# The gate product and the rotary rotation of a recurrent/attention layer given from GpSimd to VectorE

## The reference

```python
# recurrent branch, for each of two directions
r = sigmoid(einsum(xc, w_r) + b_r)            # xc: 4-tap convolution of x_rnn
i = sigmoid(einsum(xc, w_i) + b_i)
log_a = -8 * r * softplus(-lam);  a = exp(log_a)
u = sqrt(-expm1(2 * log_a)) * (i * xc)        # "gate times input" is i * xc
h = linear_scan(a, u)                         # h[t] = a[t] * h[t-1] + u[t]
# attention branch: 12 heads of 64; the first 16 columns of each head of q and k are rotated
rotated = concat([t1 * c - t2 * s, t2 * c + t1 * s])      # t1, t2: 8 columns each
```

## Time and profile before

| | us |
|---|---|
| median of 3 runs | 1599.41 |
| profiled execution, its own time | 1598.67 |
| its span, first to last instruction | 1596.9 |
| TensorE matmuls busy | 1550.0 (97%) |
| VectorE busy | 848.5 (53%) |
| ScalarE busy | 476.2 (30%) |
| GpSimd busy | 58.3 (4%) |
| mean granted clock of TensorE | 0.993 |

### The profile page before, as it was taken

One profiled execution on the slowest core, in us unless ns is written; L12 is line 12 of the kernel. 1 busy time (PEld: TensorE's weight loads), 2 busy tenths in 40 slices (PEclk: granted clock), 3 DMA queues, 4 the chain that ended last, 5 costly groups with the idle time before them and its releaser, 6 DMA issues.

```text
span 1596.9 us, 29275 instructions
## 1 busy us (share of the span) xinstructions
PE 1550.0 (97%) x12168; PEld 848.9 (53%) x12168; DVE 848.5 (53%) x1762; ACT 476.2 (30%) x699; POOL 58.3 (4%) x43
## 2 busy tenths in 40 slices
PE   6999999999999989999999999999999999999997
PEld 5877788888887877853433333333333333333332
DVE  5877676556687766744534345246245344443352
ACT  5577665444456966420000000000000000000001
POOL 0130000000003200010000000000000000000000
PEclk9999999999999999999999999999999999999998
DMA  9434365544443333559999999999999999999994
GB/s 385 152 145 149 115 226 189 205 184 184 185 172 132 136 155 108 199 197 416 399 384 425 408 386 410 404 386 420 395 402 416 371 423 415 382 414 412 384 409 188
DMA packets 66960, 473.78 MB, mean 297 GB/s; under 512 B 7408, under 2 KB 7664, under 8 KB 10768
## 3 DMA queue, kind: packets, MB, share of 16 engines
q1 hardware_dynamic: 64480, 460.88, 72.8%
q0 software_dynamic: 1920, 10.09, 1.8%
q10 hardware_dynamic: 432, 0.96, 0.2%
HBM read 469.80 MB, written 2.10 MB: 296 GB/s over the span
## 4 chain that ended last, share of the span: by engine, by line
PE 80%; DVE 9%; ACT 7%; issue 3%; DMA 1%; SPq 0%; DVEq 0%; ACTq 0%
PE bank L1298 26%; PE turn L1310 12%; PE mid L1298 10%; PE turn L1316 6%; PE bank L512 5%; PE bank L514 5%; PE bank L513 5%; DVE w_lo L507 2%; PE mid L512 2%; PE mid L514 2%; PE mid L513 2%; ACT w_hi L500 2%; DVE xT L1558 1%; DMA raw<-in_stream 1%; PE mid L1138 1%
## 5 line engine op out<-in xcount | busy, mean ns | idle before, releaser
L1298 PE MATMUL bank<-raw,gT 128*32 128x512 f32 (+1 forms) x4096 | 439.0, 566 | 0.7 <-ACT gT L957 0.7
L507 DVE TENSOR_TENSOR w_lo<-raw,w_hi 128x1024 fp32r<-128x1024 f32 x202 | 254.0, 1268 | 153.6 <-ACT w_hi L500 151.8
L1298 PEld LDWEIGHTS bank<-raw,gT 128*32 128x32 f32 x4096 | 135.4, 110 | 275.6 <-issue 266.4
L512 PE MATMUL bank<-w_hi,a_hi 128*128 128x512 f32 (+1 forms) x608 | 242.4, 399 | 15.2 <-DVE w_lo L507 12.0
L500 ACT ACTIVATE w_hi<-raw 128x1024 fp32r<-128x1024 f32 x202 | 211.2, 1056 | 127.3 <-PE bank L514 81.1
L514 PE MATMUL bank<-w_hi,a_lo 128*128 128x512 f32 (+1 forms) x608 | 234.9, 386 | 0.0
L513 PE MATMUL bank<-w_lo,a_hi 128*128 128x512 f32 (+1 forms) x608 | 234.6, 386 | 0.0
L1774 DVE STREAM_TRANSPOSE hT<-eh 32x128 f32<-32x128 f32 (+1 forms) x768 | 219.8, 286 | 24.2
L1310 PE MATMUL turn<-raw,hT 128*32 128x512 f32 x1792 | 213.1, 592 | 0.0
L1298 PE MATMUL mid<-raw,gT 128*32 128x256 f32 (+1 forms) x2048 | 189.0, 486 | 0.0
L983 ACT ACTIVATE eh<-bank 128x512 f32<-128x512 f32 (+1 forms) x32 | 17.4, 544 | 546.9 <-PE bank L1298 318.6
(11 more groups left out here) (240 smaller groups left out, 1323.7 us busy)
## 6 DMA issues: line engine op xcount, KB each, us to landing
raw<-in_stream SPq DMA_DIRECT2D x436, 1024.0 KB, 7.2
wg<-in_gates POOLq DMA_DIRECT2D x2, 2048.0 KB, 10.5
gain<-in_norms POOLq DMA_DIRECT2D x4, 512.0 KB, 4.1
x<-in_x SPq DMA_DIRECT2D x2, 512.0 KB, 6.5
raw<-in_stream SPq DMA_DIRECT2D x2, 512.0 KB, 6.5
tokens<-xs POOLq DMA_DIRECT2D x1, 1024.0 KB, 4.3
out_x<-xn SPq DMA_DIRECT2D x4, 256.0 KB, 2.2
const<-in_consts ACTq DMA_DIRECT2D x1, 752.0 KB, 11.6
```

The source lines that it names most:

```text
L507: nc.vector.tensor_tensor(w_lo[:, h % H, :], raw[:, part % R, lo:lo + HALF], w_hi[:, h % H, :].bitcast(F32), ALU.subtract).then_inc(lo_rea ...
L512: nc.tensor.matmul(out_, s_hi, wh, start=start, stop=False)
L1298: ins = nc.tensor.matmul(bank_[strip(s_), 0:w], gT[:, kt, strip(t_)], w_c, start=kt == 0, stop=kt == KT - 1)
```

## The change

The product `ig * xc` leaves GpSimd and becomes a step `lx` of VectorE. It stands at gaps 8.5, 11, 14.5 and 17 (with `le`, and half a gap later in the third block). The rotation becomes three steps of VectorE: two products at gap 11, two at 11.5, the subtraction and the addition at 14. The semaphores that were waited for by GpSimd are waited for by VectorE. GpSimd keeps its loads. Each operation keeps its shape.

```diff
@@ schedule
-        at(10, ("evac", ("qkv", 2)), ("rope",))
+        at(10, ("evac", ("qkv", 2)))
+        for i, gap in enumerate((11, 11.5, 14)):
+            at(gap, ("rope", i))
...
             at(tanh, ("la", d, hf))
+            at(decay + (d == 1 and hf == 0) / 2, ("lx", d, hf))
             at(decay, ("le", d, hf))
@@ gpsimd block
-                elif s[0] == "la":
-                    _, L, d, hf = s
-                    n = slice(4 * hf, 4 * hf + 4)
-
-                    pool.wait_ge(mid_free, mid_before(L, d * 4 + 2 * hf + 1)[1] + 4)
-                    nc.gpsimd.tensor_tensor(ig[:, n, :], ig[:, n, :], xc[:, n, :],
-                                            ALU.mult).then_inc(ix_ready, 1)
-                elif s[0] == "rope":
...
-                    for o, (a, c) in zip(tmp, ((t1, cb), (t2, sb_), (t2, cb), (t1, sb_))):
-                        nc.gpsimd.tensor_tensor(o, a, c, ALU.mult).then_inc(rope_s, 1)
-                    pool.wait_ge(rope_s, 4 * (L + 1))
-                    nc.gpsimd.tensor_tensor(t1, tmp[0], tmp[1], ALU.subtract).then_inc(rope_done, 1)
-                    nc.gpsimd.tensor_tensor(t2, tmp[2], tmp[3], ALU.add).then_inc(rope_done, 1)
@@ vector block
+                elif kind == "lx":
+                    _, L, d, hf = s
+                    n = slice(4 * hf, 4 * hf + 4)
+                    dve.wait_ge(mid_free, mid_before(L, d * 4 + 2 * hf + 1)[1] + 4)
+                    nc.vector.tensor_tensor(ig[:, n, :], ig[:, n, :], xc[:, n, :], ALU.mult).then_inc(ix_ready, 1)
+                elif kind == "rope":
+                    _, L, i = s
+                    z = qk[:, :, :].rearrange("p b (h w) -> p b h w", w=DH)
+                    NH = QK // DH
+                    t1, t2 = z[:, :, :, 0:8], z[:, :, :, 8:16]
+                    cb = cos.rearrange("p b (o k) -> p b o k", o=1).to_broadcast([P, TB, NH, 8])
+                    sb_ = sin.rearrange("p b (o k) -> p b o k", o=1).to_broadcast([P, TB, NH, 8])
...
+                    if i == 0:
+                        for n in range(3):
+                            evacuated(dve, (L, ("qkv", n)))
+
+                        bank_read(dve, TURN[("tx", L, 1)] + 1)
+                        bank_read(dve, TURN[("tx", L, 1)])
+                    if i < 2:
+                        for o, (a, c) in list(zip(tmp, ((t1, cb), (t2, sb_), (t2, cb), (t1, sb_))))[2 * i:2 * i + 2]:
+                            nc.vector.tensor_tensor(o, a, c, ALU.mult).then_inc(rope_s, 1)
+                    else:
+                        dve.wait_ge(rope_s, 4 * (L + 1))
+                        nc.vector.tensor_tensor(t1, tmp[0], tmp[1], ALU.subtract).then_inc(rope_done, 1)
+                        nc.vector.tensor_tensor(t2, tmp[2], tmp[3], ALU.add).then_inc(rope_done, 1)
```

More of the change, by code:

```diff
@@ L1535, in _ @@
                                 dve.wait_ge(chain, links[0])
+                elif kind == "lx":
[10 more added lines that the diff above has]
+                    sb_ = sin.rearrange("p b (o k) -> p b o k", o=1).to_broadcast([P, TB, NH, 8])
+                    flat = xn[:, :, :].rearrange("p b w -> p (b w)")
+                    W = TB * NH * 8
+                    tmp = [flat[:, j * W:(j + 1) * W].rearrange("p (b h k) -> p b h k", b=TB, k=8)
+                           for j in range(4)]
+                    if i == 0:
[10 more added lines that the diff above has]
+                        nc.vector.tensor_tensor(t2, tmp[2], tmp[3], ALU.add).then_inc(rope_done, 1)
                 elif kind == "lb":
```

## The result

| | before | after |
|---|---|---|
| median, us | 1599.41 (6 runs) | 1588.97 (6 runs, 1587.20 to 1589.35) |
| ratio, 95% interval | | 0.9930 (0.9917 to 0.9943) |
| profiled execution, its own time | 1598.67 | 1588.84 |
| its span | 1596.9 | 1587.0 |
| VectorE busy | 848.5 | 841.9 |

The changed kernel is 10.4 us faster by the medians and 9.9 us by the two spans; 9.8 were forecast. Lines of VectorE's code have moved: the forward scans are line 1562 now, the backward ones 1566, `w_lo` is 510, `root` 1547.

A forecast was written before the change was run, and what follows sets the result against it. A chain of waits between engines was taken to bound each layer's recurrence, TensorE the stage after. Savings of 4.76 and 5.01 us, together 9.77, with additions covered, gave a median of 1589.6 us; range for 8 in 10: 1586.5 to 1593.5.

The forecast's parts named there:

- Who makes the scans long: Recurrence: GpSimd's SBUF reads and VectorE's two-input instructions exclude each other; four forward scans take 4.65 us, backward ones 2.43.
- Removed: VectorE's excess leaves the chain: first scans 2.28, ScalarE's wait 0.18 or 0.43, second scans 2.16, third block's `root` 0.14 us.
- Added: New VectorE work per layer: four gate products at 1.225 us and six rotation operations on 384 elements at 0.55 us.
- The scattered row: VectorE row with a scattered operand, 0.40 us above the plain one; its share would make a rotation operation 0.85 us.
- GpSimd's price: Rival, rotation dear on VectorE: at GpSimd's 1.30 us each 1592.0 us, at 1.87 each 1596.6 us; chance 0.07.
- Where it lies: Each addition was held against VectorE's idle time at its own place; nothing was forecast to come onto the chain.
- The place forecast as tight: Gaps 11 and 11.5, ahead of the second block's `root`: 3.0 us added, 2.1 us or more of idle time left.
- What is late next: TensorE's second wait for a `w_lo`, at 136.43 before, was to stay about 1.9 to 2.2 us.
- TensorE is beside this chain: Recurrence: TensorE's waits of 3.53 and 1.85 us for a `w_lo` behind scans were taken as off the chain.
- the second way of reckoning: TensorE's saving per layer: 3.0 us of waiting plus 1.3 of clock, 4.3 us and a rest, near the 4.8.
- half of the 9.8 us given back: Rival: a slow-clock stretch or wait hidden by the old stall takes about half the gain: 1593.5 us, chance 0.08.
- Time: Whole kernel: profiled execution from 1598.67 to 1588.9 us, median from 1599.41 to 1589.6 us, VectorE's busy time falling.

The follow-up runs named there:

- e3: The changed kernel plus GpSimd products that nothing reads, at the places where its work stood: 1599.07 us, ratio to the kernel before 0.9996.
- e4: The changed kernel plus GpSimd fills of an unused tile with a constant, which read nothing from SBUF: 1587.33 us, ratio to the kernel before 0.9924.
- e9: The kernel before, all arithmetic still on GpSimd, with waits that start its work when VectorE has little to do: 1588.90 us, ratio 0.9935.
- e2: The kernel before with only the gate products moved to VectorE, the rotation staying on GpSimd at gap 10: 1599.19 us, ratio 0.9995.
- e5: The changed kernel with all six rotation operations in one piece at gap 10, ahead of the first block's scans: 1599.60 us, ratio 0.9998.
- e8: The changed kernel with each block's scans at the gap of its second product, ahead of a `w_lo`: 1596.90 us, ratio to the kernel before 0.9985.
- e10: The changed kernel with the third block's scans half a gap later, behind one more `w_lo`: 1592.45 us, ratio to the kernel before 0.9956.

## Why the prediction was right

- *Who makes the scans long.* Shown: 670 ns without GpSimd in all sixteen, 1224 before, stretched again by products that nothing reads (e3), not by fills (e4), and not when the same work comes later (e9).
- *Removed.* The four terms were 2.28, 0.18 or 0.43, 2.16 and 0.14 us. Measured from `root` to `root`, first to second block: 21.45 to 18.88 in the first layer (2.57, forecast 2.46) and 21.68 to 18.87 in the second (2.81, forecast 2.71); second to third block: 23.37 to 21.08 and 23.38 to 21.08 (2.29 and 2.30, forecast 2.30); third to fourth block 17.11 to 17.14. Each layer is right to 0.1 us.
- *Added.* 0.55 us for an operation on 384 elements and 0.47 from start to start were taken; 0.552 was measured, and two take 1.02. So runs of 8 cost nothing extra here; the reason given for it was not tried. The scattered row and GpSimd's price were too high as bounds.
- *Where it lies.* All additions were covered. The place forecast as tight had 2.23 us left, for "2.1 us or more".
- *What is late next.* TensorE's waits were forecast at 0.4 to 0.5 and 1.9 to 2.2 us and came at 0.50 and 1.81. But the sentence "TensorE is beside this chain" was wrong for the kernel before. TensorE's path was only 0.5 us shorter, and the second way of reckoning, which came to nearly the same sum, should have been a warning. The change frees both paths, but not by the same: from the first `root` on, TensorE's matmuls for the third block's sigmoids end 4.29 us earlier than before (the prediction had 4.3 and a rest), while ScalarE comes to them 4.73 us earlier (first layer). The matmuls then end only 0.1 us ahead of their reader. The prediction held no row for this margin; that it was just enough was luck. The reading failed as soon as I used it for a part (e2) or for another order (e5, e8): the expectations there were wrong by 4.4, 5 and 13 to 17 us.
- *Read or added up wrong, without consequence.* "Each `w_lo` that meets GpSimd is longer" does not hold: the pair at 60.70 takes 2.36 us in the kernel before, as without GpSimd, under a gate product drawn from 58.70 to 65.30; there GpSimd stood still (see the last section). The four rows of `w_lo` hold 4.4 us of excess, not 4.7. And half of the 9.8 us given back would make 1594.5 us, not 1593.5.
- *Time.* The span was forecast to fall by 9.77 us and fell by 9.9. The median fell by 10.44, which the uncertainty of the ratio, 0.13%, covers.

## What to carry to other kernels

An instruction that the profile draws at twice the length of its twins may be waiting inside itself; before blaming its form, look at what GpSimd does in those microseconds, and whether it reads SBUF. Moving such GpSimd work in time can be worth as much as moving it to another engine. And before a gain on a chain is counted, look for the second path that is about as long: a cure that frees both pays in full, and one that frees only one may pay nothing.

## What the runs showed of the hardware

GpSimd loses as well when VectorE has no gap. Its gate product takes 2.40 us alone, but 6.60 in the earlier trace rows and 6.62 in e9 at 58.79, while VectorE issues without a break. GpSimd gets through at last when VectorE comes to a pair of the convolution, which is then drawn to 2.81 us (e9 at 63.09) from 0.75 in the change. That pair has one tile and a column of factors as inputs. So it isn't shown that only VectorE's instructions with two tiles as inputs are held up.

TensorE's clock also makes a difference that is nobody's work. Behind each recurrence there is a short stretch that some executions run at the lower of the two clock levels (1.2 GHz) for a part, and others don't. First layer, the change (first row) and e4 (second row), whose instructions of TensorE are the same:

```profile
150.00:155.00 5.00, 4.30 (x14) 3.52 (x15) 3.42 (x4) 0.75 (x1) 0.00 (x0) 0.66 0.93 338
```

```profile
150.00:155.00 5.00, 3.96 (x23) 3.44 (x24) 3.76 (x5) 1.64 (x3) 0.00 (x0) 1.00 0.83 311
```

The granted clock is 0.66 over these 5 us in one and 1.00 in the other. From the fourth `root` of the first layer to the first `root` of the second it is 364.74 us in the change and 363.15 in e4; both have the same 57.1 before and after. A profiled execution can carry one such stretch in either layer, or both, as e10 does (364.68 us between the layers, and 1026.5 from the last `root` to the end for 1024.9 in the change). That is 1.6 to 1.7 us each, and accounts for the 1.7 us that e10's span has above its 2.3 (that all six runs of e10 took 1591.17 us or more suggests that it comes more often there, which was not followed up); the 1.6 us that e9's span is shorter than the change's is one such stretch. The kernel before had one too, behind the second layer (1026.7 us to the end, but 363.15 between the layers), so that it cancels in the comparison of the two spans.

What decides whether it comes was not tried, but the traces limit it. In the change's first layer TensorE is busy for only 1.16 of the 3 us from 147 to 150, just ahead of the stretch. In e4 it is busy for 2.95 there: its clock had already fallen at 132 to 138 us (0.78 and 0.65), behind TensorE's second wait, where the loss changes no distance, and it did not fall again. A pause of TensorE alone is not enough, though. e9 has the same one (1.00 of 3 us), and its granted clock stays at 1.00 both behind the second wait and behind the pause.
